# Squares summed on GpSimd ahead of the norm statistics, with a reordered first stage, a moved pair of staging tiles and a merged last norm

## What is computed

```python
for i in range(2):
    x = x + 0.5 * swiglu(rmsnorm(x, norm_ffn[i, 0]), w_gate_up, w_down)      # D_FF = 2816
    h = rmsnorm(x, norm_mix[i])
    x = x + (even_mixer(h) if i == 0 else odd_mixer(h))
    x = x + 0.5 * swiglu(rmsnorm(x, norm_ffn[i, 1]), w_gate_up, w_down)
    gate = sigmoid(rmsnorm(x, norm_ple[i]) @ w_ple_gate[i])
    x = x + gate * rmsnorm(p[i] @ w_ple_proj[i], norm_ple_proj[i])
y = rmsnorm(x, norm_final)
# rmsnorm: x * rsqrt(mean(x * x, axis=-1) + 1e-6) * g
```

## Time and profile before

| | us |
|---|---|
| time, median of 3 runs | 2807.28 (2678.33 to 2918.97) |
| the profiled execution | 2676.04 |
| its span on the slowest core | 2674.5 |
| spans of the 8 cores | 2663.4 to 2674.5 |
| TensorE busy | 2610.7 (98%) |
| VectorE busy | 1161.5 (43%) |
| ScalarE busy | 750.2 (28%) |
| GpSimd busy | 290.8 (11%) |
| granted TensorE clock, mean of a core | 0.992 to 0.994 |

### The profile page before, as it was taken

One profiled execution on the slowest core, in us unless ns is written; L12 is line 12 of the kernel. 1 busy time (PEld: TensorE's weight loads), 2 busy tenths in 40 slices (PEclk: granted clock), 3 DMA queues, 4 the chain that ended last, 5 costly groups with the idle time before them and its releaser, 6 DMA issues.

```text
span 2674.5 us, 34780 instructions; the slowest of 8 cores (2663.4 to 2674.5 us)
## 1 busy us (share of the span) xinstructions
PE 2610.7 (98%) x14264; PEld 1272.2 (48%) x14264; DVE 1161.5 (43%) x1978; ACT 750.2 (28%) x1306; POOL 290.8 (11%) x406
## 2 busy tenths in 40 slices
PE   7899999999999999999999999999999999999997
PEld 2454444445454544444444444444444454444443
DVE  3332232586852523226732324247665324232376
ACT  2211101354851111125631010133224311101265
POOL 2100000002400000001600000000000000000034
PEclk9899999999999999999999999999999999999998
DMA  8132221034233221231031222111311322222103
GB/s 198 24 52 34 38 39 28 22 49 92 50 61 51 44 33 32 35 53 30 14 59 32 38 38 36 25 25 24 65 33 28 70 40 34 34 37 40 32 9 134
DMA packets 60815, 120.97 MB, mean 45 GB/s; under 512 B 8816, under 2 KB 29424, under 8 KB 60656
## 3 DMA queue, kind: packets, MB, share of 16 engines
q0 software_dynamic: 34560, 92.42, 21.1%
q1 hardware_dynamic: 26096, 26.33, 3.3%
HBM read 197.00 MB, written 11.18 MB: 78 GB/s over the span
## 4 chain that ended last, share of the span: by engine, by line
PE 90%; DVE 7%; ACT 2%; DMA 1%; issue 1%; POOL 0%; SPq 0%; DVEq 0%; ACTq 0%; POOLq 0%
PE ps L496 90%; DVE h L475 2%; DVE scr L468 1%; DVE x L475 1%; ACT L459 1%; DVE x L468 1%; ACT scr L459 0%; DVE scr L475 0%; DMA o_pool_s<-xo 0%; DVE v L1031 0%; DVE v L468 0%; ACT nrs L459 0%; DMA x<-xT 0%; DVE us L475 0%; DVE pb L475 0%
## 5 line engine op out<-in xcount | busy, mean ns | idle before, releaser
L496 PE MATMUL ps<-h,ring 128*128 128x512 bf16 (+1 forms) x9120 | 1713.4, 349 | 17.2 <-DVE h L475 11.9
L496 PEld LDWEIGHTS ps<-h,ring 128*128 128x128 bf16 x9120 | 820.1, 98 | 890.1 <-DVE h L475 23.6
L459 ACT ACTIVATE scr<-ps 128x512 f32<-128x512 f32 (+1 forms) x673 | 356.3, 534 | 1539.7 <-PE ps L496 1526.7
L496 PE MATMUL ps<-hid,ring 128*128 128x512 bf16 (+1 forms) x3840 | 712.5, 347 | 5.0 <-ACT scr L459 2.6
L468 DVE TENSOR_TENSOR hid<-ps,scr 128x512 bf16<-128x512 f32 (+1 forms) x440 | 269.1, 612 | 981.8 <-PE ps L496 976.1
L496 PEld LDWEIGHTS ps<-hid,ring 128*128 128x128 bf16 x3840 | 344.4, 98 | 371.3 <-ACT scr L459 3.6
L475 DVE SCALAR_TENSOR_TENSOR x<-ps,x 128x512 f32<-128x512 f32 (+1 forms) x480 | 283.9, 609 | 282.5 <-PE ps L496 280.1
L516 POOL DMA_DIRECT2D ring<-wts x233 | 123.6, 536 | 2238.8 <-PE ps L496 2160.2
L475 DVE SCALAR_TENSOR_TENSOR h<-x,par,nrs 128x512 bf16<-128x512 f32 (+1 forms) x320 | 226.4, 753 | 65.6 <-ACT nrs L459 65.6
L459 ACT ACTIVATE h<-x 128x512 bf16<-128x512 f32 (+1 forms) x248 | 135.5, 566 | 166.4 <-DVE x L475 115.4
L468 POOL TENSOR_TENSOR x<-x,scr 128x512 f32<-128x512 f32 (+1 forms) x80 | 101.9, 1286 | 80.1 <-DVE scr L475 80.0
(11 more groups left out here) (75 smaller groups left out, 587.5 us busy)
## 6 DMA issues: line engine op xcount, KB each, us to landing
ring<-wts POOLq DMA_DIRECT2D x92, 512.0 KB, 5.1
ring<-wts POOLq DMA_DIRECT2D x64, 256.0 KB, 4.9
ring<-wts POOLq DMA_DIRECT2D x64, 224.0 KB, 4.1
ring<-wts POOLq DMA_DIRECT2D x12, 768.0 KB, 8.7
x<-xT SPq DMA_DIRECT2D x32, 256.0 KB, 5.7
yT<-x SPq DMA_DIRECT2D x32, 256.0 KB, 2.0
ys<-yst SPq DMA_DIRECT2D x32, 68.0 KB, 2.5
pt<-pT POOLq DMA_DIRECT2D x4, 544.0 KB, 16.2
```

The source lines that it names most:

```text
L459: S.op("act", lambda e: e.activation(out=out, in_=in_, func=func, **kw), reads=rd, writes=[out])
L496: ins = e.matmul(ps_ap, l, r, start=st, stop=sp)
```

## The change

- `square_sum` replaces `square` at the ends of the four feed-forwards and of the odd mixer. In a large block ScalarE writes tile 0's square into an f32 tile `ACC[b % 2]` and the others into scratch; GpSimd adds them one by one (7 adds), the last one into `H[:, 0]` in bf16. `stats` then has one matmul (`nsq=1`). The small block stays as it was. These norms are pushed with a delay of 9 instead of 2, and large blocks tick once per item instead of twice.
- `ACC` lies over `PB`, `STP0`, `PTAIL` and `O_DP`, all of the even mixer; the memset of `PTAIL` moves behind the first feed-forward.
- The first part of the first feed-forward takes tiles 0 and 1 of a block together from block 2 on, and pushes block 3's norm after item 14 and block 4's after item 16.
- `uf0` gets bytes of its own, and the other staging tiles move into those of `STP`.
- In the last embedding stage the addition to x is on VectorE, squares follow one item later, the norm of a block is pushed after item 1 of the next, and those of blocks 3 and 4 come together at the end, with both statistics ahead of the scales. An Ln on one column is put in before the last squares.

```diff
-    for i_, o_ in enumerate((z3, z0 + 2 * 15 * NS * 4, z0 + 2 * 15 * NS * 4 + 1024)):
-        UFX.append((alloc(f"uf{i_}", [128, 128], F32, at=o_), alloc(f"xo{i_}", [128, 128], F32, at=o_ + 512)))
+    uf0_off = cur[0]
+    cur[0] += 512
+    st_b = 15 * NS * 4
+    for i_, (o_, o2_) in enumerate(((uf0_off, z0 + 2 * st_b), (z0 + 3 * st_b, z0 + 3 * st_b + 512),
+                                    (z0 + st_b, z0 + st_b + 512))):
+        UFX.append((alloc(f"uf{i_}", [128, 128], F32, at=o_), alloc(f"xo{i_}", [128, 128], F32, at=o2_)))
...
+    acc_off = cur[0]
+    PB = [alloc(f"pb{i}", [128, 512], BF16) for i in range(NPB)]
+    STP0 = alloc("stp0", [128, 15 * NS], F32)
     PTAIL = alloc("ptail", [128, 4, 16], F32)
...
+    ACC = [alloc(f"acc{i}", [128, 512], F32, at=acc_off + i * 2048) for i in range(2)]
...
-            (mm_split if split else mm_group)(pb[:, 0:n], [(ONES[:, :], SQ[:, c, c0:c0 + n]) for c in range(8)])
+            (mm_split if split else mm_group)(pb[:, 0:n], [(ONES[:, :], SQ[:, c, c0:c0 + n]) for c in range(nsq)])
...
+    def square_sum(SQ, c, b):
+        if b == SB:
+            return square(SQ, c, b)
+        c0, n = BLOCKS[b]
+        acc = ACC[b % 2][:, 0:n]
+        if c == 0:
+            act(acc, X[:, c, c0:c0 + n], AF.Square)
+        else:
+            t = scratch()
+            act(t[:, 0:n], X[:, c, c0:c0 + n], AF.Square)
+            tt("pool", acc if c < 7 else SQ[:, 0, c0:c0 + n], acc, t[:, 0:n], ALU.add)
...
     def late_loads():
+        dve_memset(PTAIL[:, :, :], 0.0)
...
-                order += [(t, b) for t in range(nt) for b in range(2, NB)]
+                order += [(t, b) for b in range(2, NB) for t in range(2)]
+                order += [(t, b) for t in range(2, nt) for b in range(2, NB)]
...
-                    for b_ in {1: (1,), 12: (2,), 16: (3, 4)}.get(oi, ()):
+                    for b_ in {1: (1,), 12: (2,), 14: (3,), 16: (4,)}.get(oi, ()):
...
                         dn_item(mo, b)
-                        square(H, mo, b)
-                        tick(2, 1)
+                        square_sum(H, mo, b)
+                        tick(1 if b < SB else 2, 1)
...
-                    push_norm(b, next_g, H)
+                    push_norm(b, next_g, H, delay=9.0, nsq=1 if b < SB else 8)
...
+        fin = next_g == "norm_final"
+        lag = 1 if fin else 3
...
-                tt("pool", X[:, mo, c0:c0 + n], X[:, mo, c0:c0 + n], t1[:, 0:n], ALU.add)
+                tt("dve" if fin else "pool", X[:, mo, c0:c0 + n], X[:, mo, c0:c0 + n], t1[:, 0:n], ALU.add)
                 sqq.append((mo, b))
-                if len(sqq) > 3:
+                if len(sqq) > lag:
                     square(HID, *sqq.pop(0))
...
+                if fin:
+                    if mo == 1 and 0 < b < NB - 1:
+                        push_norm(b - 1, next_g, HID, delay=1.0)
+                    if b == NB - 1 and mo == 7:
+                        act(RC[:, 15:16], RC[:, 0:1], AF.Ln)
+                    tick(2, NB)
...
+        if fin:
+            push_norm(NB - 2, next_g, HID)
+            push_norm(NB - 1, next_g, HID)
+            i_ = [i for i, st in enumerate(pend) if st[3]]
+            pend.insert(1, pend.pop(i_[1]))
```

More of the change, by code:

```diff
@@ L409, in build_program @@
     RC = alloc("rc", [128, 16], F32)
+    ZTAIL = alloc("ztail", [128, 8, 2], F32)
+    NPB = 3
+    acc_off = cur[0]
+    PB = [alloc(f"pb{i}", [128, 512], BF16) for i in range(NPB)]
+    STP0 = alloc("stp0", [128, 15 * NS], F32)
     PTAIL = alloc("ptail", [128, 4, 16], F32)
-    ZTAIL = alloc("ztail", [128, 8, 2], F32)
-    STP0 = alloc("stp0", [128, 15 * NS], F32)
     O_DP = alloc("o_dp", [128, 4, 30], F32)
-    NPB = 3
-    PB = [alloc(f"pb{i}", [128, 512], BF16) for i in range(NPB)]
+    ACC = [alloc(f"acc{i}", [128, 512], F32, at=acc_off + i * 2048) for i in range(2)]
+    assert acc_off + 4096 <= cur[0]
     SCW = 528
@@ L599, in tick, with push_norm @@
             _run(pend.pop(0))
-    def push_norm(b, gname, SQ, delay=2.0, split=False, own=False):
+    def push_norm(b, gname, SQ, delay=2.0, split=False, own=False, nsq=8):
         c0, n = BLOCKS[b]
@@ L614, in push_norm @@
         tag = (stage[0] - own, b)
-        pend.append([tag, pet[0] + delay, stats])
+        pend.append([tag, pet[0] + delay, stats, True])
         def mk(c):
@@ L624, in push_norm @@
         for c in range(8):
-            pend.append([tag, 0.0, mk(c)])
+            pend.append([tag, 0.0, mk(c), False])
     def square(SQ, c, b):
@@ L645, in build_program @@
         dve_memset(RC[:, t:t + 1], 1.0 / (t + 1))
-    dve_memset(PTAIL[:, :, :], 0.0)
     dve_memset(ZTAIL[:, :, :], 0.0)
@@ L1123, in ple @@
                     W.done(("pleg", l, mo))
-                if b and mo == 3:
-                    push_norm(b - 1, next_g, HID, delay=4.0 if b < NB - 1 else 1.0)
-                tick(2, NB if next_g == "norm_final" else 1)
+                if fin:
[4 more added lines that the diff above has]
+                    tick(2, NB)
+                else:
+                    if b and mo == 3:
+                        push_norm(b - 1, next_g, HID, delay=4.0 if b < NB - 1 else 1.0)
+                    tick(2, 1)
             if b == NB - 1:
@@ L1129, in ple @@
                     square(HID, *sqq.pop(0))
-        push_norm(NB - 1, next_g, HID, delay=1.0)
+        if fin:
[3 more added lines that the diff above has]
+            pend.insert(1, pend.pop(i_[1]))
+        else:
+            push_norm(NB - 1, next_g, HID, delay=1.0)
         W.done(("plep", l))
```

## The result

The changed kernel takes 2650.76 us, the median of five runs (fastest 2649.55), against 2678.33 of before beside it (fastest 2677.77): a ratio of 0.9897 with a 95% interval of 0.9884 to 0.9911. The gain is 27 us where 59 was forecast, and the time lies 15 us above the top of the range.

What follows compares the result with a forecast made beforehand. TensorE, busy 2610.7 of 2674.5 us, was taken as the bound; 30.1 + 1.3 + 14.5 + 7.9 + 5.9 - 1.0 = 58.7 us off gave a span of 2615.8, forecast 2617 us, range 2608 to 2636.

Steps and rivals of the forecast that it cites:

- start: First feed-forward's start: reordered items and earlier norms remove two TensorE stops and the half clock behind; gain 14.5 us.
- staging tiles: Even mixer: with uf0 and xo0 elsewhere, VectorE no longer waits for a transfer, nor TensorE for VectorE; gain 7.9 us.
- end: Last embedding stage: additions on VectorE and both last norms at the very end; gain 5.9 us (bounds 2 and 9).
- sums, with the waits before them: Five stage ends: 140 fewer ones-matmuls, 30.1 us, plus 1.3 us of TensorE's waits before statistics.
- what the adds cost: Weight load queued behind GpSimd's adds at the first feed-forward's end costs 1.0 us; VectorE's lag costs TensorE 0.
- TensorE sets the pace there, so this is gained in full: Five stage ends: the 30.1 us of removed ones-matmuls all shorten the span unless a wait takes their place.
- VectorE falls some 3 us behind: Feed-forward ends: scales and adds taking turns need 29.2 us against TensorE's 26.1.
- TensorE stands still only at about 10 us: Feed-forward ends: with 8 PSUM banks, one per item, VectorE's lag stops TensorE only at that size.
- I take 1.0 us (0 to 6): Even mixer's weights: load leaves 0.6 to 3.5 us later behind the adds, most of TensorE's wait recovered; loss 1.0 us.
- Rival 2: The port makes TensorE wait at four feed-forward ends, price 12 to 22 us, so 2629 to 2639; chance 0.17.
- Rival 3: One of three stalls (start, mixer's front, end) returns in another form, 6 to 15 us, 2623 to 2632; chance 0.17.
- Rival 4: At stage ends, update x<-ps,x also takes turns with the adds, 48 us, so 2665; chance 0.04.

Runs made afterwards that it cites:

- e2: Changed kernel without the GpSimd sums: eight squares and eight ones-matmuls per block, delay 2 and two ticks back at the five ends; 2655.84 us, fastest of four runs.
- e3: Changed kernel with the 140 GpSimd adds left out, the one ones-matmul summing a single square (norm values wrong); 2635.08 us, ratio 0.9845.
- e6: Changed kernel with block 3 of the first feed-forward left unsummed (eight squares, eight ones-matmuls); 2645.63 us, ratio 0.9857.
- e8: Changed kernel with block 1's norm held back to the next stage at the five ends; 2677.71 us, ratio 0.9989.
- e7: Changed kernel with sums of two tiles only, four adds and four ones-matmuls per large block; 2647.59 us median, ratio 0.9867.

## Why the prediction was wrong

The sum was 58.7 us, and the spans differ by 25.7 (2674.5 to 2648.8). The 33.0 us between are found, on the slowest core of each kernel:

| term | forecast | measured | from |
|---|---|---|---|
| start | 14.5 | 13.65 | e2 against before, first two rows |
| staging tiles | 7.9 | 8.1 | e2 against before |
| end | 5.9 | -1.05 | e2 against before |
| sums, with the waits before them | 31.4 | 22.2 without adds | e3 (core 3) against e2, spans |
| what the adds cost | -1.0 | -16.7 | after against e3 (core 3), spans |

(The measured terms come to 26.2; the 0.5 us beyond the difference of the spans lie in stages that no term speaks of.)

- **Start: right**, mechanism and size. (The 0.077 us taken for a small matmul is the busy time of eight over eight; their starts are 0.056 apart. That moves the sum by 0.5 us.) **Staging tiles: right** for the slowest core; the work it frees is taken at VectorE's pace, as worked out. But the 6.00 us for which VectorE waited for the transfer were the longest of the eight cores (1.4 to 6.0), and so the gain in this stage is 1.1 to 8.1 us by core. That the core that was read is also the one that sets the time is what makes the sum come out.
- **"TensorE sets the pace there, so this is gained in full": wrong for 9.2 us.** It was said of five stage ends, but half of the statistics, those of blocks 2 and 3, are due in the next stage. At the head of the even mixer and of both embedding stages TensorE waits for VectorE, so taking its work away there gives nothing: e3 got -0.45, 0.5 and 0.5 us of 3.0 each, which is 8.5 of the 9.2. In the first of them the statistics also stood between the release of the ring's room and the first use of the new weights; with one block's statistics left in place, 1.5 us of matmuls, the wait for the ring is 0.74 us (e6), and without them 2.30 (e3). The trace of before said it: the earlier trace rows gives VectorE 58 of 72 us in that front, and TensorE's waits for `scr` were in its list.
- **"VectorE falls some 3 us behind" and "TensorE stands still only at about 10 us": wrong, about 2 us at four ends.** Both the lag and the slack were mis-sized, and the slack decided it. The lag is 4.1 us. It rises by 1.5 us at block 0's first scale and by 1.2 at block 1's, as the next update stands behind that scale in VectorE's order and the scale waits for Ln and Exp on ScalarE (1.66 and 1.31 us): a wait that the prediction put at nothing. It falls by 1.1 at the one item without a scale, and grows by 2.5 over the others. Only these 2.5 are the collision that was worked out, and with 0.66 + 1.24 = 1.90 us for a scale and an add in turn, where the rows have 1.68 us for the whole item; that the forecast said 3 is in part luck. The slack of 10 us was reckoned in large items. Eight banks are eight items, and in the small block an item comes every 0.39 us, so eight banks last 3.1 us, less than the lag. The table has the loss as after against e3: 2.4, 1.9, 1.9 and 2.1 us. e8, with half of the scales, and e7, with fewer adds, have no such stops.
- **"I take 1.0 us (0 to 6)" for the late weights: wrong, 5.2 us** (138.49 against 133.26), near the end of the bounds that was not taken. Several things met. The load was issued 5.25 us later than without adds (526.19 against 520.94), as the small block's stops were in the way as well. It took 12.35 us from issue to use, 3.6 more than e3's 8.7, because `STP0` lies in `ACC`'s bytes: its load, and the copies behind it on SP's queue, waited for the same add and left together with the weights. The prediction asked what is behind the adds on GpSimd's queue and did not ask it of SP's. So TensorE waits 4.4 us more for the ring than in e3 (6.73 against 2.30). The stage's first 16 matmuls, behind the small block's stops, run at the lower level: from the first to the next operation it is 5.06 us instead of 3.45. And "most of it comes off the 3.05 us it waits for VectorE" did not hold: only 0.9 us came off (0.34 us for `pb` against e3's 1.24). The 5.2 us are the slowest core's; the others lose 1.6 to 4.6.
- **"Gain 5.9 us" at the end: wrong, a loss of 1.** Its item was VectorE's, "2.6 us against 2.94 before", and measured 2.65. But 2.94 was the time of the items in which two scales met an add, not of all, and the step did not set 2.6 beside TensorE's 2.155: the addition was moved from an idle engine to the one that becomes the bound. The sum had no term for the body of the stage, and the body grew from 78.8 us (2567.55 to 2646.39) to 84.0 (2539.59 to 2623.62), with 14 ones-matmuls less in it: TensorE waits for `scr`, and twice 1.05 us for the last square before a norm's statistics, a wait that e2 has too. And the tail is 25.2 instead of 22.2: the last square came 12.5 us behind the small block's first item, not 8.9, as its items wait 1.9 and 0.9 us for VectorE and then run at half the clock.
- **Not told apart:** 3.2 of the 16.7 us that the adds cost lie in the two embedding stages (82.90 against 81.38, 109.21 against 107.51), behind the ends at which VectorE is late. No run says which wait carries them.
- **Rivals.** Rival 2 had the right mechanism and place; its price of 12 to 22 us was above the 8.3 that the four ends lost. Rival 3 named the end as one of its three. Both came true at once, with the loss in the stage heads, which no rival held, and the late weights beyond their 1.0. The signs of being wrong that it named, waits for `x<-ps,x` and for the ring at a stage's end and a clock under 1 there, are the ones that came. The chances were written as if one excluded the other. Rival 4 is refuted: updates stay at 0.68 us beside adds (678 ns mean of 17, against 685 of 15 before).
- The Trainium skill ("SBUF — State Buffer", Who interferes with whom) says that the shared ports are held for a whole instruction against a VectorE operation with two SBUF inputs. The trace agrees as to what is touched: the scale is 1.12 us in the mean beside adds and 0.74 without, the update from PSUM is untouched. Its strict reading, an item of 2.28 us, is not what the trace shows (1.68 us an item).

## What to carry to other kernels

Work taken from the engine that is busy 98% of the time is a gain only where that engine ends the wait; ask it of every place where the work is issued, stage heads included, and not of the stage that the edit is written in. Slack in buffers is so many items, not so many microseconds: price it at the shortest item that follows. And when a tile is laid over another's bytes, follow what waits for them on every DMA queue, for a load held back holds back whatever stands behind it.

## What the runs showed of the hardware

- An f32 add of 128x512 on GpSimd takes 1.27 us (median; 1263 to 1537 ns over 120), and a 0.74 us scale on VectorE takes 1.12 us in the mean beside such adds (0.74 to 1.50, mostly 1.16). The engine's idle time was no measure of what it costs: 183 us more of GpSimd's time (421.7 against 238.9 in e2) cost 15.7 us of the whole.
- Loads and DRAM-to-DRAM copies that leave together slow each other, by about what each would take alone. The 704 KB copy landed after 7.2 to 7.4 us away from the loads and 23.9 us beside 2.4 MB of them (two of 768 KB, and 512, 320 and 64), which without the copies landed in up to 15.8 us (e6). The weights, issued first, came into use after 12.35 us with the copies beside them and after 9.7 with the copies sent first.
- A stop costs more than itself, since TensorE's clock is at its lower level for a time (granted 0.82 from 516 to 540 us), and not in proportion to its length: behind ring waits of 2.30, 3.97, 4.08 and 6.73 us the 24 matmuls took 7.04, 7.04, 8.23 and 6.82 us, behind those of 0.57 and 0.74 us 5.35.
